# Running sums of the decays of the first mixer: rows through a scratch tensor in DRAM in place of products on TensorE

## The reference, cut to what matters

```python
dt = softplus(dt_raw + dt_bias).reshape(bsz, nc, Q, G, K)      # Q = 128 tokens, G*K = 2*8 heads
a = dt * (-exp(a_log)).reshape(G, K)
a_cum = cumsum(a, axis=2)                                      # running sum over a chunk
seg = a_cum[:, :, :, None] - a_cum[:, :, None, :]              # (l, s) for every head
decay = exp(where(causal, seg, -inf))
cb = einsum('bclgn,bcsgn->bclsg', cm, bm)
y_diag = einsum('bclsg,bclsgk,bcsgkp->bclgkp', cb, decay, xdt)
```

## Time and profile before

| | |
|---|---|
| median of 3 runs | 1268.45 us (1268.35 to 1268.46) |
| the profiled execution | 1268.46 us, of which the span (first to last instruction) is 1266.7 us |
| PE busy | 1255.7 us (99%) |
| DVE, ACT, POOL busy | 908.2, 721.5, 104.9 us |
| granted TensorE clock | 0.999 of full speed |
| DMA | 224.42 MB, mean 177 GB/s |

### The profile page before, as it was taken

How to read it: one execution, slowest core, us unless ns; L and a number is a source line. 1 busy time by engine, 2 the same in 40 slices (tenths; PEclk the granted TensorE clock), 3 DMA queues, 4 the chain that set the end, 5 groups by cost and what they waited for, 6 DMA issues and landing times.

```text
span 1266.7 us, 17805 instructions
## 1 busy us (share of the span) xinstructions
PE 1255.7 (99%) x7056; PEld 1090.1 (86%) x7056; DVE 908.2 (72%) x1283; ACT 721.5 (57%) x1059; POOL 104.9 (8%) x137
## 2 busy tenths in 40 slices
PE   9999999999999999999999999999999999999997
PEld 8998778888888988888888888888888998888886
DVE  6967655777776685776666867877777897766665
ACT  5865454655555684754545545555555875654553
POOL 2000000000000440000000000000000781000000
PEclk9999999999999999999999999999999999999999
DMA  8443226466663313355554643686564533455551
GB/s 293 167 168 133 100 100 212 154 226 222 225 221 132 139 53 114 133 199 199 200 196 170 212 164 133 231 302 228 214 218 171 195 113 133 167 202 203 196 183 64
DMA packets 32802, 224.42 MB, mean 177 GB/s; under 512 B 3776, under 2 KB 4160, under 8 KB 7248
## 3 DMA queue, kind: packets, MB, share of 16 engines
q1 hardware_dynamic: 32576, 223.22, 50.0%
q10 hardware_dynamic: 144, 0.07, 0.0%
HBM read 222.23 MB, written 1.05 MB: 176 GB/s over the span
## 4 chain that ended last, share of the span: by engine, by line
PE 98%; DVE 1%; DMA 0%; ACT 0%; issue 0%; POOL 0%; ACTq 0%; SPq 0%; DVEq 0%; POOLq 0%
PE pb L496 24%; PE pb L467 16%; PE pb L468 16%; PE pb L469 16%; PE pb L501 13%; PE pb L473 3%; PE pb L1052 2%; PE pb L566 1%; PE pb L863 1%; PE pb L887 1%; PE pb L568 1%; PE pb L627 1%; PE pb L639 1%; PE pb L1111 0%; DMA xt<-d_x 0%; PE pb L694 0%
## 5 line engine op out<-in xcount | busy, mean ns | idle before, releaser
L1681 DVE TENSOR_TENSOR wlo<-raw,whi 128x2048 fp32r<-128x2048 f32 (+2 forms) x194 | 428.0, 2207 | 184.7 <-ACT whi L1165 184.3
L1165 ACT ACTIVATE whi<-raw 128x2048 fp32r<-128x2048 f32 (+1 forms) x196 | 371.9, 1899 | 63.3 <-PE pb L469 57.3
L496 PE MATMUL pb<-both,whi 128*128 128x512 f32 x1344 | 321.2, 391 | 0.0
L496 PEld LDWEIGHTS pb<-both,whi 128*128 128x128 f32 x1344 | 249.3, 188 | 49.9
L467 PE MATMUL pb<-whi,both 128*128 128x512 f32 (+2 forms) x728 | 285.6, 392 | 0.0
L468 PE MATMUL pb<-wlo,both 128*128 128x512 f32 (+2 forms) x728 | 281.6, 387 | 0.0
L469 PE MATMUL pb<-whi,both 128*128 128x512 f32 (+2 forms) x728 | 281.3, 386 | 0.0
L1168 ACT ACTIVATE arena<-pb 128x256 f32<-128x256 f32 (+1 forms) x234 | 95.7, 422 | 229.2 <-PE pb L501 149.3
L501 PEld LDWEIGHTS pb<-both,wlo 128*128 128x128 f32 x1344 | 172.3, 191 | 6.5
L501 PE MATMUL pb<-both,wlo 128*128 128x256 f32 x1344 | 174.3, 283 | 0.0
L469 PEld LDWEIGHTS pb<-whi,both 128*128 128x128 f32 x728 | 136.7, 188 | 27.9
(11 more groups left out here) (159 smaller groups left out, 1192.5 us busy)
## 6 DMA issues: line engine op xcount, KB each, us to landing
raw<-d_ws SPq DMA_DIRECT2D x198, 1024.0 KB, 4.9
raw<-d_ws SPq DMA_DIRECT2D x5, 768.0 KB, 4.3
arena<-d_diag SPq DMA_DIRECT2D x4, 960.0 KB, 7.6
raw<-d_ws SPq DMA_DIRECT2D x2, 576.0 KB, 3.7
arena<-d_c SPq DMA_DIRECT2D x1, 1060.0 KB, 5.0
xt<-d_x SPq DMA_DIRECT2D x2, 512.0 KB, 4.5
raw<-d_ws SPq DMA_DIRECT2D x2, 512.0 KB, 7.6
arena<-d_rows SPq DMA_DIRECT2D x2, 512.0 KB, 6.1
```

The source lines that it names most:

```text
L496: e.matmul(bs[i][:, :], wh[:, k, 128 * i:128 * i + 128], both[:, k, :], start=k == 0, stop=k == 7, skip_group_check=True)
L1165: e.activation(split_parts(n)[0], raw_part(n), ACT.Copy).then_inc(*sig("act.hi", f"hi{n}"))
L1681: e.tensor_tensor(l[:, a:b], raw_part(n)[:, a:b], f32(h[:, a:b]), ALU.subtract).then_inc(*sig("dve.lo", f"lo{n}"))
```

## The change

The running sums are computed once for all 32 columns in row form and come to the partitions by DMA:

- PE: beside the product that gives the column form (L723 before), a second one, with `a` as the stationary operand, gives a 32x128 block with one row for each chunk and head (L722 after). The 32 products at L627 and their eight bank claims are gone; what is left of PE's `decays` is `pairing(c, g)`, the `cb` product.
- DVE copies the block into `glT` after the `gk` products have read that tile, ACT stores it (16 KB) into the new DRAM tensor `acum` and goes on.
- SP loads `acum` twice, 16 rows of it (8 KB) to each of 128 partitions, 1 MB each time: chunk c = 1 in front of the load of weight chunk 12, c = 0 in front of that of weight chunk 14, each behind the wait for the store, the second also behind `conv2`. They land in the room of `zs` and `gs`, which are written by the gates later.
- DVE's `decays(n)` reads those rows instead of a PSUM bank.

```diff
@@ -211,6 +211,7 @@
         self.M = room(1536, 3)
         self.pv = room(1024, 2)
         self.cb4 = room(128)
+        self.rows = (cut(self.gs.rearrange("p a b -> p (a b)"), 16), cut(self.zs.rearrange("p a b -> p (a b)"), 16))
         self.glT = room(256)
         small = room(32 * 14)
         self.w2 = room(512)
...
@@ -406,6 +407,12 @@
             sp_load(e, "c0", c0[:, 128:NC0], d_c0[:, 128:NC0])
             sp_load(e, "w2", ssd.w2[0:16, :], d_gkw2)
             for p, n in enumerate(ORDER[3:], 3):
+                if n in (12, 14):
+                    c = int(n == 12)
+                    e.wait_ge(*at("acum.out"))
+                    e.wait_ge(*at("xT0.3" if c else "conv2"))
+                    sp_load(e, f"acum{c}", ssd.rows[c].rearrange("p a b -> p (a b)"),
+                            d_acum[16 * c:16 * c + 16, :].rearrange("(o a) b -> o (a b)", o=1).to_broadcast([P, 2048]))
                 if n == CHUNK["w_ukv", 1]:
                     e.wait_ge(*at("x2.11"))
                     sp_load(e, "c1", mla.c1[:, :], d_c1)
...
@@ -613,20 +620,11 @@
                         m = tr(b[:, 128 * i:128 * i + 128], T.xbc[:, 4 * c + i, 3 + 128 * t:131 + 128 * t])
                     m.then_inc(*sig(key, f"xsT{t}{c}"))
 
-                def decays(n, spot=None):
-                    c, g, hh = SSD_UNITS[n]
-                    if hh == 0:
-                        b = claim(f"cb{c}{g}")
-                        cs = slice(3 + 128 * c, 131 + 128 * c)
-                        e.matmul(b[:, 0:128], T.xbc[:, 8 + g, cs], T.xbc[:, 10 + g, cs], start=True,
-                                 stop=True).then_inc(*sig(key, f"cb{c}{g}"))
-                    b = claim(f"dec{n}", spot)
-                    e.wait_ge(*at("a"))
-                    for i in range(4):
-                        h = 16 * c + 8 * g + 4 * hh + i
-                        m = e.matmul(b[:, 128 * i:128 * i + 128], T.a[:, h:h + 1].to_broadcast([P, P]), UM,
-                                     start=True, stop=True)
-                    m.then_inc(*sig(key, f"dec{n}"))
+                def pairing(c, g):
+                    b = claim(f"cb{c}{g}")
+                    cs = slice(3 + 128 * c, 131 + 128 * c)
+                    e.matmul(b[:, 0:128], T.xbc[:, 8 + g, cs], T.xbc[:, 10 + g, cs], start=True,
+                             stop=True).then_inc(*sig(key, f"cb{c}{g}"))
 
                 def outputs(n):
                     c, g, hh = SSD_UNITS[n]
...
@@ -720,7 +718,8 @@
                         b = claim("acol")
                         e.wait_ge(*at("a"))
                         e.wait_ge(*at("in.c0"))
-                        e.matmul(b[:, 0:32], UM, T.a, start=True, stop=True).then_inc(*sig(key, "acolm"))
+                        e.matmul(b[:, 0:32], UM, T.a, start=True, stop=True)
+                        e.matmul(b[0:32, 128:256], T.a, UM, start=True, stop=True).then_inc(*sig(key, "acolm"))
                 for i in range(4):
                     stationary(key, 7 + i, claim(f"kq{i}"), f"kq{i}")
                     if i == 2:
...
@@ -736,9 +735,10 @@
                 for c in range(2):
                     bs = [claim(f"v{c}.{t}") for t in range(2)]
                     moving(key, 11 + 2 * c, bs, 512, 0)
-                    decays(0) if c == 0 else (outputs(0), decays(2))
+                    pairing(0, 0) if c == 0 else (outputs(0), pairing(0, 1))
                     moving(key, 12 + 2 * c, bs, 512, 4, f"vm{c}")
-                    decays(1) if c == 0 else (outputs(1), decays(3))
+                    if c == 1:
+                        outputs(1)
                 def turn(j):
                     kt = 2 * j if j < 4 else 2 * (j - 4)
                     src = T.gs if j < 4 else T.zs
...
@@ -751,7 +751,7 @@
                     if c < 3:
                         outputs(2 * c + 2)
                     if c < 2:
-                        decays(2 * c + 4)
+                        pairing(1, c)
                     if c == 0:
                         kend_turn()
                     elif c == 1:
...
@@ -766,12 +766,10 @@
                     if c < 3:
                         outputs(2 * c + 3)
                     if c == 0:
-                        decays(5)
                         scores()
                     elif c == 1:
                         states(1)
                         head(0, 4)
-                        decays(7, 5)
                     elif c == 2:
                         states(3)
                         head(2, 4)
...
@@ -1269,6 +1267,8 @@
                     if j == 5:
                         e.wait_ge(*at("acol"))
                         run(key, "eac", T.eac, T.acol, ACT.Exp)
+                        e.wait_ge(*at("acum"))
+                        e.dma_start(d_acum, T.glT[0:32, 0:128]).then_inc(*sig("act.acum", "acum.out", by=16))
                         e.wait_ge(*at("U2"))
                         run(key, "U3", T.U, T.U, ACT.Ln)
                 for i, dst in enumerate((T.k, T.k, T.q, T.q)):
...
@@ -1782,14 +1782,14 @@
 
                 def decays(n):
                     c, g, hh = SSD_UNITS[n]
-                    e.wait_ge(*at(f"dec{n}"))
+                    e.wait_ge(*at(f"in.acum{c}"))
                     if n >= 3:
                         e.wait_ge(*at(f"y{n - 3}"))
                     own()
                     for i in range(4):
                         h = 16 * c + 8 * g + 4 * hh + i
-                        ts(key, [f"d{n}", f"dec{n}.gone"], T.M[:, n % 3, 128 * i:128 * i + 128],
-                           bank(f"dec{n}")[:, 128 * i:128 * i + 128], T.acol[:, h:h + 1], ALU.subtract, 0.0, ALU.min)
+                        ts(key, [f"d{n}"], T.M[:, n % 3, 128 * i:128 * i + 128], T.rows[c][:, h - 16 * c, :],
+                           T.acol[:, h:h + 1], ALU.subtract, 0.0, ALU.min)
 
                 def masked(n):
                     c, g, hh = SSD_UNITS[n]
...
@@ -1885,7 +1885,9 @@
                         stt(key, ["U0"], T.U, T.X, -1.0, T.X, ALU.mult, ALU.min)
                     if j == 4:
                         e.wait_ge(*at("acolm"))
-                        copy(key, ["acol", "acol.gone"], T.acol, bank("acol")[:, 0:32])
+                        copy(key, ["acol"], T.acol, bank("acol")[:, 0:32])
+                        e.wait_ge(*at("gk"))
+                        copy(key, ["acum", "acol.gone"], T.glT[0:32, 0:128], bank("acol")[0:32, 128:256])
                         own()
                         ts(key, [], T.X, T.X, 0.0, ALU.min)
                         e.wait_ge(*at("U1"))
```

More of the change, by code:

```diff
@@ L104 @@
 DIAG_LOADS = tuple(f"diag{i}" for i in range(4))
-LOADS = DIAG_LOADS + ("x0", "x1", "half1", "c0", "cols", "w2", "c1", "c2", "pw", "pos", "rows", "fg")
+LOADS = DIAG_LOADS + ("acum0", "acum1", "x0", "x1", "half1", "c0", "cols", "w2", "c1", "c2", "pw", "pos", "rows", "fg")
 class Tally:
@@ L313, with build @@
 OUT_SLOTS = ((1, 2), (3, 4), (8, 9), (10, 11))
-def build(nc, d_x, d_ws, d_cols, d_c0, d_c1, d_c2, d_gkw2, d_poolw, d_rows, d_pos, d_diag, d_out):
+def build(nc, d_acum, d_x, d_ws, d_cols, d_c0, d_c1, d_c2, d_gkw2, d_poolw, d_rows, d_pos, d_diag, d_out):
     ctx = ExitStack()
@@ L342, in build @@
         keys = [f"{e}.{s}" for e in ("pe", "act", "dve", "pool") for s in STAGES]
-        keys += ["act.hi", "dve.lo"] + [f"sp.raw{i}" for i in range(NR)] + [f"sp.{n}" for n in LOADS] + ["sp.out", "act.ident"]
+        keys += ["act.hi", "dve.lo"] + [f"sp.raw{i}" for i in range(NR)] + [f"sp.{n}" for n in LOADS] + ["sp.out", "act.ident", "act.acum"]
         tally = Tally({k: ctx.enter_context(nc.semaphore("s_" + k.replace(".", "_"))) for k in keys})
@@ L2714 @@
     out = nc.dram_tensor("out", (1, 256, 1024), F32, kind="ExternalOutput").ap()
-    build(nc, *args, out)
+    acum = nc.dram_tensor("acum", (32, 128), F32, kind="Internal").ap()
+    build(nc, acum, *args, out)
     r = _run(nc, [arrays], core_ids=[0])
```

## The result

| | before | after |
|---|---|---|
| median | 1268.43 us (1268.15 to 1268.64, 11 runs) | 1271.69 us (1270.42 to 1272.89, 11 runs) |
| ratio | | 1.0025, 95% interval 1.0016 to 1.0034 |
| profiled execution | 1268.46 us, span 1266.7 | 1270.42 us, span 1268.6 |

What follows compares the result with a forecast made beforehand. The prediction took PE, busy 99% of the span, as the bound. Removed products -6.9, row product +0.2 and waits +7.1 gave +0.4 us on 1268.45, forecast 1268.8 us, range 1264.5 to 1272.0.

Steps and rivals of the forecast that it cites:

- the likeliest case (no difference): Whole kernel: 1268.8 us, within 0.2% (2.5 us) of before; forecast chance 0.66, chance of the same time 0.70.
- edge of 1271.0: Whole kernel: a time over 1271.0 us counts as slower by over 0.2%, given a chance of 0.17.
- rival B: At chunk 21, the clock falls in the third wait, up to +5.5 us: 1271.5 to 1274.3 us; chance 0.09.
- upper edge of 1272.0: Whole kernel: top of the stated range, which starts at 1264.5 us and leaves out about 0.2 of the chances.
- D: At the masked products, DVE's `lo` work becomes the bound and PE waits 1 to 3 us: 1269.8 to 1271.8; chance 0.06.
- The removed products: On PE, eight groups of running sums go, 0.81 to 0.99 us each, together 6.9 us.
- The row product: On PE beside the column form, one product of two instructions adds 0.2 us, bounds 0 and 0.4.
- The four waits: PE waits at `head(0)` 1.65 us, `head(2)` 1.27, chunk 21 3.07, output product 0.94; with semaphores 7.1.
- The edges of its own range: Removed products 6.5 to 7.3 us and waits 6.4 to 7.6, giving the forecast's own range of 1267.7 to 1269.9.
- rival A: At the four new PE waits: they are hidden and the removed products stay a gain, 1263.5 us; chance 0.14.
- DVE, ACT, SP, DMA at nothing: Added copy, store, SBUF reads and two loads of rows on the other engines cost 0.
- C: At chunk 12 behind the first load, rows come late and PE loses about 7 us: 1275.8; chance 0.05.
- By the rows none: Behind the third wait, at chunk 21: no loss from a lower clock, taken as 0.

Runs made afterwards that it cites:

- e2_first: Changed kernel with head 2 in bank 5 and the second bank of the last z columns in bank 2, leaving only the first wait; 1265.18 us.
- e7_second: Changed kernel with head 0 in bank 5 and the second bank of the last z columns in bank 2, leaving only the second wait; 1263.26 us.
- e4_before_third: Kernel before, all products left in, with head 2 claiming bank 3 instead of bank 4; 1274.54 us, ratio 1.0046.
- e8_third: e1_ring with head 2 in bank 2, so only the third wait is there; 1267.06 us.
- e5_no_rows: e1_ring without the store of the running sums and without the two loads of rows; 1261.99 us.
- e1_ring: Changed kernel with the ring stepping past seven banks, so later claims have the banks of the kernel before; 1261.83 us, ratio 0.9946.
- e3_not_first: Changed kernel with head 0 in bank 5, so only the first wait goes and the second to fourth stay; 1269.12 us.

## Why the prediction was right and where it was wrong

The time, 1271.69 us, lies in the range, but near its upper end, and the likeliest case (no difference) was the wrong one: by the prediction's own edge of 1271.0 this is slower, and its own sign for rival B, a PEclk under 1.00 behind 135 us, came. That the range holds it is in part luck. Its upper edge of 1272.0 was drawn to take in all of D, which didn't come, and only a part of B. The time also lies inside what B gave, 1271.5 to 1274.3, but B had worked that out from a loss at chunk 21, where the profiled execution lost nothing. By its steps:

- **The removed products**: 6.9 worked out. PE was 0.39 late behind the row product and 5.84 ahead at `off0`, so seven groups gave 6.23; the eighth gives 0.91, 7.14 in all. The 0.2 missing is time that a group costs its neighbours, which I had left out: the `cb` product in front of the first group took 0.22 (81.47 to 81.69) and takes 0.14 (81.86 to 82.00) without it, and the chunk product behind the second took 0.31 (88.86 to 89.17) where the others take 0.23.
- **The row product**: 0.2 taken, 0.44 measured in the trace, a little over the upper bound of 0.4.
- **The four waits**: 1.7, 1.3, 3.1 and 1.0 expected in the list of what would show it; measured, by how far PE fell back at each place, 1.70, 1.32, 3.16 and 0.97, together 7.15 for 7.1. e2_first and e7_second show the first and the second alone as the cost of a bank number, e4_before_third the second and third together, and e8_third the third; the fourth was never made alone. This is the step that carried the rest, and rival A, its opposite, is refuted. The ring is seven claims short and not eight, but the table of banks was right, and the waits were worked out from that.
- **The edges of its own range**: 6.4 and 7.6 for the waits are wider than what the terms give (6.93 with 0 to 0.5 on top), and the low edge comes to 1268.45 - 7.3 + 6.4 = 1267.6 and not 1267.7. Neither matters for the result. The 2.5 us of "no difference" were wider than the noise: the kernel before is spread over 0.5.
- **DVE, ACT, SP, DMA at nothing**: right. e5_no_rows shows it for the DMAs. The loads took 7.3 us, between the 4.9 and the 12.2 of the bounds. The slack held them: ACT reads chunk 12 at 70.50 with them (e1_ring) and at 70.53 without (e5_no_rows). DVE's four reads take 0.87 where they took 1.12, within the bounds. Rivals C and D did not come.
- **"By the rows none"**: this is the step that failed. I set the clock's cost to 0 because no row of before showed a lower level, but no row of before showed a wait over 1.2 us either, so the rows could not tell. Rival B had the mechanism and too small a chance (0.09), and it was tied to the third wait only; in the profiled execution the clock fell behind the first, of 1.64 us, and held behind the third. The sum without the clock is 1268.43 - 7.14 + 0.44 + 7.15 = 1268.9, 0.1 from the forecast, and none of the eleven executions reached it: the profiled one is 1270.42 - 1268.9 = 1.5 above, one fall (1.54 by the head's duration), and the median 2.8. One more execution is like the profiled one (1270.44, clock 0.998). The other nine were not traced; their clocks of 0.995 to 0.997, and times at least 1.0 us longer, speak for a longer fall or a second one.

On an otherwise full PE the clock fell at a gap of 1.64 us that stands alone in four of six executions (e2_first: by the mean clock of each, one of them with a trace), and a gap of 1.24 left it up in five of five (e7_second). The Trainium skill (TensorE: Matmul & The Clock Gate, HAM oscillation) says that gaps between matmuls let the clock fall. The direction agrees. But the page speaks of longer gaps than any here, so the prediction's "by that rule there would be a loss" took more from it than it says, and the measurement, a fall behind 1.64 us, goes beyond the page.

What stays open: why the same wait is followed by a fall in one execution and not in the next, whether the small products ahead of the first wait take part in it, and which waits the untraced executions of the changed kernel fell behind. No kernel here parts that.

## What to carry to other kernels

Where buffers are handed out in turn, an edit that drops a few claims moves every later claim to another tenant: list claim, bank and tenant before and after, and ask of each tenant when its last reader is done. Here four claims got a tenant that was not yet done, which took back the whole gain, and passing over seven banks gave it back. Where PE is busy throughout, a new wait of the size seen here (1.64 us and more) has to be priced with the clock behind it, even where the trace before has never shown a fall; between 1.24 and 1.64 us nothing was measured.

## What the runs showed of the hardware that was not expected

- PE at half the clock lost 1.54 us behind a wait of 1.64 (the head's 3.96 us for 2.42), and 2.9 us behind a wait of 3.0 in e8_third, where the clock was low from 159.8 to 166.6. The fall can cost nearly as much as the wait itself.
- It is a matter of the execution: the same kernel shows groups of times that are 1.6 us apart in e2_first and 1.3 or more in e3_not_first, so a median over few executions can land in either.
- A load in which 128 partitions read the same 8 KB lands in 7.3 us, against 4.9 for as many bytes from a weight chunk; SP had issued a chunk's load 0.4 us before the first (53.19 and 53.61) and 1.2 before the second (64.44 and 65.64), and how much of the 7.3 belongs to that is not parted.
